# Second layer of a two-layer attention and expert backbone: units ordered by token group, vector work placed inside the attention stream

## The reference, cut to what matters

```
# modulation: m = silu(cond) @ w_mod + b_mod, six rows of 1024 per group
q, k, v = split(h @ w_in_c)                  # 1024 -> 1024 | 256 | 256
q, k = rms_norm per head of 64               # 16 query heads, 4 key heads
# g = 1 only: rotary on q and k; 128 cached keys and values are appended
o = softmax(q k^T / 8) v                     # g = 0: 128 keys, g = 1: 256 keys
x = layer_norm(ALPHA * x + gate * (o @ w_out_c))
h = modulate(x)                              # then router, 16 experts, top 2
y = sum over experts of gate_e * (silu(h w_gate) * (h w_up)) w_down
```

## Time and profile before

| | us |
|---|---|
| median of 3 runs | 865.54 (863.39 to 866.21) |
| the profiled execution | 865.44 |
| its span, first to last instruction | 863.6 |
| TensorE busy in it | 775.2 (90%) |
| VectorE busy | 233.3 (27%) |
| ScalarE busy | 151.4 (18%) |
| mean granted TensorE clock | 0.962 of full |
| transfers | 287.37 MB, 333 GB/s over the span |

### The profile page before, as it was taken

One profiled execution on the slowest core, in us unless ns is written; L12 is line 12 of the kernel. 1 busy time (PEld: TensorE's weight loads), 2 busy tenths in 40 slices (PEclk: granted clock), 3 DMA queues, 4 the chain that ended last, 5 costly groups with the idle time before them and its releaser, 6 DMA issues.

```text
span 863.6 us, 9955 instructions
## 1 busy us (share of the span) xinstructions
PE 775.2 (90%) x3765; PEld 371.1 (43%) x3765; DVE 233.3 (27%) x531; ACT 151.4 (18%) x389; POOL 63.3 (7%) x126
## 2 busy tenths in 40 slices
PE   4799788999999998797899996999999999997794
PEld 1345444546543443243234644554744434442331
DVE  0004444445210100000345055455610110000046
ACT  0211332213200111011112113233311101110120
POOL 0000000001100011001000030000200001101000
PEclk9898799999999999999999996999999999999998
DMA  8989940189999999999999899521099999999971
GB/s 312 382 311 401 389 152 31 68 307 404 419 419 417 420 419 417 419 422 414 417 386 384 321 353 420 227 98 64 35 370 417 420 416 419 421 415 418 419 321 50
DMA packets 78525, 287.37 MB, mean 333 GB/s; under 512 B 6508, under 2 KB 12140, under 8 KB 62100
## 3 DMA queue, kind: packets, MB, share of 16 engines
q1 hardware_dynamic: 74452, 275.60, 80.6%
q10 hardware_dynamic: 2880, 7.03, 2.1%
q0 software_dynamic: 1152, 4.19, 1.2%
HBM read 278.99 MB, written 7.82 MB: 332 GB/s over the span
## 4 chain that ended last, share of the span: by engine, by line
PE 50%; SPq 30%; DMA 7%; DVE 7%; issue 2%; ACT 2%; POOL 1%; ACTq 0%; DVEq 0%
SPq L580 15%; PE bank L1001 10%; SPq L575 9%; PE bank L748 9%; PE bank L837 6%; DMA ring<-in_exp_w_up 5%; SPq L576 4%; PE bank L1035 4%; PE bank L785 3%; PE bank L675 3%; DMA ring<-in_w_mod 2%; PE bank L654 2%; PE bank L972 2%; PE bank L816 2%; PE bank L794 2%
## 5 line engine op out<-in xcount | busy, mean ns | idle before, releaser
L1001 PE MATMUL bank<-ring,arena 128*64 128x512 f32 x1024 | 231.4, 605 | 30.1 <-DMA ring<-in_exp_w_up 29.2
L1001 PEld LDWEIGHTS bank<-ring,arena 128*64 128x64 f32 x1024 | 75.4, 139 | 182.8 <-issue 151.3
L1035 PE MATMUL bank<-ring,arena 128*64 128x512 f32 x512 | 113.8, 596 | 5.9 <-DMA ring<-in_exp_w_down 4.9
L1542 DVE TENSOR_TENSOR arena<-bank,arena 128x256 f32<-128x256 f32 x32 | 13.6, 424 | 253.6 <-ACT arena L1697 253.6
L748 PE MATMUL bank<-ring,arena 128*128 128x512 f32 (+2 forms) x224 | 75.4, 499 | 1.1 <-ACT arena L1631 1.1
L1621 ACT ACTIVATE arena<-bank 128x512 f32<-128x512 f32 (+6 forms) x79 | 41.0, 539 | 159.2 <-PE bank L748 66.9
L1035 PEld LDWEIGHTS bank<-ring,arena 128*64 128x64 f32 x512 | 36.1, 137 | 71.9 <-issue 64.6
L972 PE MATMUL bank<-arena 128*128 128x128 f32 x512 | 62.2, 275 | 0.0
L837 PE MATMUL bank<-ring,arena 128*128 128x512 f32 x128 | 60.3, 605 | 0.0
L972 PEld LDWEIGHTS bank<-arena 128*128 128x128 f32 x512 | 59.6, 192 | 1.3 <-issue 1.0
L675 PE MATMUL bank<-ring,cwin 128*32 128x512 f32 x384 | 48.2, 652 | 10.8 <-DMA ring<-in_w_mod 10.8
(11 more groups left out here) (168 smaller groups left out, 610.5 us busy)
## 6 DMA issues: line engine op xcount, KB each, us to landing
ring<-in_exp_w_gate SPq DMA_DIRECT2D x64, 1024.0 KB, 19.8
ring<-in_exp_w_up SPq DMA_DIRECT2D x64, 1024.0 KB, 20.6
ring<-in_exp_w_down SPq DMA_DIRECT2D x64, 1024.0 KB, 25.0
ring<-in_w_mod SPq DMA_DIRECT2D x24, 2048.0 KB, 18.2
expert_rows<-arena ACTq DMA_DIRECT2D x12, 512.0 KB, 7.8
ring<-in_w_out_ab SPq DMA_DIRECT2D x2, 2048.0 KB, 20.6
ring<-in_w_in_c SPq DMA_DIRECT2D x2, 2048.0 KB, 23.8
ring<-in_w_out_c SPq DMA_DIRECT2D x2, 2048.0 KB, 12.9
```

The source lines that it names most:

```text
L1001: mm = nc.tensor.matmul(pb(key)[SLOTS * hf:SLOTS * (hf + 1), :], xeT[b][:, k * P + SLOTS * a:k * P + SLOTS * (a + 1)], w[:, :, k % 4, hf * ...
L1035: mm = nc.tensor.matmul(pb(key)[SLOTS * a:SLOTS * (a + 1), :], hp[:, c:c + SLOTS], w[:, a, kf % 2, hf * HALF:(hf + 1) * HALF], start=(kf = ...
```

## The change

The second layer alone is changed; the first keeps its order.

- The units go by group: the four of g = 0 first, then the eight of g = 1.
- The projection goes by group: `project_odd` does all four blocks for g = 0, then for g = 1, so the first three blocks are given back later. The last block of g = 1 (the values) comes behind the transposes of g = 0's q and k (`odd_heads(0)`); that block is given back at the first scores.
- The two modulation pieces become four pairs (`mod_pair`), one before the first T and three behind T(1), T(2) and T(5); their closing matmul has 2 columns. Each pair gives its two ring slots back there.
- On DVE the scaling of g = 1 (`odd_scaled(1)`) stands behind T(0), the rotation, now in three pieces, behind T(1), the two residual sums of g = 0 behind T(5) and T(6), `mod_ab` and the normalisation of g = 0 behind T(7): each ahead of the next unit's maxima.
- q and k of g = 1 are turned behind T(2). The gates of g = 0 stand behind T(3) and T(4), the modulation's columns behind T(7), in bank 1, which the second residual sum has emptied. The columns of g = 0 for the router stand behind S(10) and S(11), its logits behind V(11).
- Of the four residual sums, the two of g = 1 are left behind the last Y, and the filler before the transposes there drops from five matmuls to three.

```diff
-    for pair in range((KVH_B if layer == 0 else KVH_C) // 2):
-        for g in range(G):
-            for kv in (2 * pair, 2 * pair + 1):
-                add("gqa", g, kv)
+    for g in range(G):
+        for kv in range(KVH_B if layer == 0 else KVH_C):
+            add("gqa", g, kv)
...
+    between = {0: [("n1", 0)], 1: [("mc", 1), ("n1", 1)], 2: [("mc", 2), ("g1", 0)], 3: [("gt", 0)], 4: [("gt", 1)],
+               5: [("mc", 3), ("au", 0)], 6: [("au", 1)], 7: [("mt", 0), ("nm", 0)]}
+    behind = {8: [("ht", 0)], 9: [("ht", 1)], 11: [("lg", 0)]}
     n = len(attention_units(layer))
     steps = [("S", 0), ("S", 1)]
+    if layer == 1:
+        steps.append(("mc", 0))
...
+        if layer == 1:
+            steps += between.get(u, [])
...
-        if layer == 0:
-            steps += make.get(u, [])
+        steps += (make if layer == 0 else behind).get(u, [])
...
-                for b in range(len(WIN[l])):
+                if l == 0:
+                    for b in range(len(WIN[l])):
+                        for g in range(G):
+                            t.use(("z", l, b, g), (2 * b + g) % 4)
+                    t.use(("mod", l, 1), 3)
+                else:
                     for g in range(G):
-                        t.use(("z", l, b, g), (2 * b + g) % 4)
-                t.use(("mod", l, 1), 3 - l)
-                if l == 1:
-                    t.use(("mod", 1, 2), 3)
+                        for b in range(len(WIN[l])):
+                            t.use(("z", l, b, g), b)
...
-                            t.use(("qT", 1, g, j), 4 + j)
-                    for j in range(2):
-                        t.use(("kT", 1, j), 6 + j)
+                            t.use(("qT", 1, g, j), (4 if g == 0 else 2) + j)
+                        t.use(("kT", 1, g), 6 if g == 0 else 2)
...
+                    elif name == "mc":
+                        t.use(step, 7)
+                    elif name == "gt":
+                        t.use(("gate", 1, 0, 0, u), 7)
+                    elif name == "mt":
+                        t.use(("modT", 1, 1), 1)
...
+            def project_odd():
+
+                for g in range(G):
+                    for b, (c0, c1) in enumerate(WIN[1]):
+                        if (g, b) == (1, 3):
+                            odd_heads(0)
+                        pe.wait_ge(*got(index[("win", 1, b)]))
+                        w = block_ap(index[("win", 1, b)])[:, 0:KD * (c1 - c0)].rearrange("p (k c) -> p k c", k=KD)
+                        key = ("z", 1, b, g)
+                        room(pe, key)
+                        if b == 0:
+                            pe.wait_ge(*saved(("hT", 1, 0, g, 1)))
+                            pe.wait_ge(*saved(("hT", 1, 0, g, 0)))
+                        for k in range(KD):
+                            mm = nc.tensor.matmul(pb(key)[:, 0:c1 - c0], hT[:, g, k, :], w[:, k, :],
+                                                  start=(k == 0), stop=(k == KD - 1))
+                            if (g, k) == (1, 0) and b > 0:
+                                mm.then_inc(*release(index[("win", 1, b - 1)]))
+                        mm.then_inc(*fill(key))
+
+            def odd_heads(g):
+
+                pe.wait_ge(s_zfin, 3 + g)
+                for a in range(2):
+                    transposes(("qT", 1, g, a), [z[1][:, g, (4 * a + j) * P:(4 * a + j + 1) * P] for j in range(4)])
+                keys = []
+                for a in range(2):
+                    keys.append(z[1][:, g, Z_KC + a * P:Z_KC + (a + 1) * P])
+                    if g == 1:
+                        keys.append(cache_kc[:, a * P:(a + 1) * P])
+                if g == 1:
+                    pe.wait_ge(s_cache, 96)
+                transposes(("kT", 1, g), keys)
+
+            def mod_pair(i):
+
+                key, first = ("mc", i), ODD_PAIRS[i]
+                room(pe, key)
+                out = pb(key)
+                for c in (first, first + 1):
+                    n = index[("mod", 1, c)]
+                    pe.wait_ge(*got(n))
+                    w = block_ap(n)
+                    for k in range(KD):
+                        j = k % 4
+                        mm = nc.tensor.matmul(out[32 * j:32 * j + 32, :], cwin[:, k, 24 - 2 * c:56 - 2 * c],
+                                              w[:, k * HALF:(k + 1) * HALF],
+                                              start=(c == first and k < 4), stop=False, skip_group_check=True)
+                    mm.then_inc(*release(n))
+                nothing = tri[0:DEPTH * N_MOD, 0:1].to_broadcast([DEPTH * N_MOD, 32])
+                nc.tensor.matmul(out[0:32, 0:2], nothing, rows[0:DEPTH * N_MOD, 0:2],
+                                 start=False, stop=True, skip_group_check=True).then_inc(*fill(key))
+
+            def odd_gate(hf):
+
+                pe.wait_ge(*saved(("mc", 0)))
+                mod_row(("gate", 1, 0, 0, hf), 1, 2, 0, hf)
+
+            def odd_columns():
+
+                for i in (1, 2):
+                    pe.wait_ge(*saved(("mc", i)))
+                mod_columns(1, 1)
+
...
+                    if (l, u, i) == (1, 0, 0):
+                        mm.then_inc(*release(index[("win", 1, 3)]))
...
-                        if (u, ci, hf) == (6, 0, 0):
+                        if (u, ci, hf) == (6 + 2 * l, 0, 0):
...
+                for g in range(l, G):
+                    logits(l, g)
...
-                project(l)
-                modulation(l, 1, (index[("win", l, len(WIN[l]) - 1)],))
-                if l == 1:
-                    modulation(1, 2)
+                if l == 0:
+                    project(0)
+                    modulation(0, 1, (index[("win", 0, len(WIN[0]) - 1)],))
+                else:
+                    project_odd()
...
+            def odd_rotated():
+                for h0, h1 in ((0, 8), (8, 16), (16, H_C + KVH_C)):
+                    last = rotate(halves(z[1][:, 1, h0 * HD:h1 * HD], h1 - h0), cst(C_COSB, 32), cst(C_SINB, 32),
+                                  odd_cos, odd_sin)
+                    if h1 < H_C + KVH_C:
+                        ch.then(last)
+                last.then_inc(s_zfin, 1)
+
...
+                odd_stats(0)
+                odd_scaled(0)
+                odd_stats(1)
+                odd_keys(0)
...
+                    elif name == "mc":
+                        dve.wait_ge(*full(step))
+                        if u > 0:
+                            dve.wait_ge(*saved(("mc", u - 1)))
+                        V.tensor_tensor(mods[1][:], mods[1][:], pb(step)[:], ALU.add).then_inc(*drain(step))
+                    elif name == "n1":
+                        (odd_rotated() if u else odd_scaled(1))
+                    elif name == "g1":
+                        odd_keys(1)
+                    elif name == "mt":
+                        mod_ab(1, 1)
+                    elif name == "au":
+                        add_up(1, 0, 0, u)
+                    elif name == "nm":
+                        normal(1, 0, 0)
...
                 if (l, s) == (1, 0):
-                    mod_ab(1, 1)
-                add_up(0, 0)
-                add_up(0, 1)
-                add_up(1, 0)
-                if (l, s) != (1, 1):
-                    normal(0)
-                add_up(1, 1)
+                    dve.wait_ge(s_out, 96)
+                else:
+                    add_up(l, s, 0, 0)
+                    add_up(l, s, 0, 1)
+                add_up(l, s, 1, 0)
+                if l == 0:
+                    normal(l, s, 0)
+                add_up(l, s, 1, 1)
...
+                        if g == 1:
+                            act.wait_ge(s_stat, root(("odd", 0)))
+                        for b in range(3):
                             act.wait_ge(*saved(("z", 1, b, g)))
-                        A.activation(sq[:, g].rearrange("p h c -> p (h c)"), z[1][:, g, 0:Z_VC],
+                        A.activation(sq.rearrange("p h c -> p (h c)"), z[1][:, g, 0:Z_VC],
                                      ACT.Square).then_inc(s_sq, 1)
-                    zp = z[1][:, 0, :]
-                    act.wait_ge(*saved(("z", 1, 3, 0)))
-                    act.dma_start(o_["new_gqa_v"][0, 0].rearrange("t h c -> t (h c)"),
-                                  zp[:, Z_VC:C_IN]).then_inc(s_out, 16)
+                        if g == 1:
+                            odd_queries(0)
+                        projected(1, 3, g)
```

243 lines of the change are left out of this document (131 added, 112 removed).

## The result

| | before | after |
|---|---|---|
| median of the runs | 865.88 us (4 runs) | 853.25 us (4 runs) |
| the profiled execution | 865.44 | 854.07 |
| its span | 863.6 | 852.3 |
| projection to first gate-and-up matmul | 161.50 | 147.21 |
| from there to the end of the span | 241.26 | 241.47 |

The ratio of after to before is 0.9838, with a 95% interval of 0.9805 to 0.9871. Forecast were 854.1 us and a first gate-and-up matmul near 611; it stands at 610.83.

A forecast was written before the change was run, and what follows sets the result against it. TensorE's list up to the second layer's first gate-and-up matmul was taken as the bound, with a fixed stretch behind it. 12.3 + 1.1 + 4.7 - 2.7 - 4.0 = 11.4 us gained, giving 854.1 us, range 850.5 to 860.

The forecast's parts named there:

- The frame: Second layer's first gate-and-up matmul sets the end: each microsecond earlier moves the whole remainder by one, 241 us to the end.
- The start of the attention: Second layer, before the first Y ends: waits for q, k and first softmax, and half clock, would go; gain 12.3 us.
- the closing matmuls: End of the modulation: two matmuls of 1.0 us each become four of two columns, 0.9 us together; gain 1.1 us.
- New waits: Second layer's attention: TensorE waits newly for DVE and ACT at several units; cost 4.0 us, bounds nothing to 18.7.
- The k transposes of g = 1: Behind the q transposes: TensorE waits 2.0 us for ACT's copy, held behind DVE's rotation and unit 3's exponentials.
- Y(0): First output tile, at 516.7: `w_out_c` lands at 516.3, so no wait was counted, with the cover nearly gone.
- The rival of a late weight: At the first output tile: `w_out_c` arrives late behind modulation blocks, 5 us, total 859 us; chance 0.07.
- the slow rival: Attention stream: DVE's queue becomes the bound and all 18.7 us of its work shows, total 871 us; chance 0.04.
- The end of the attention: Last Y to the transposes of g = 1: 10.87 us becomes 6.17 as two residual sums move earlier; gain 4.7 us.
- From those transposes to the experts: Transposes of g = 1 to first gate-and-up matmul, 19.2 us: led by DVE and GpSimd, so no gain counted.
- The logits: Router logits of g = 0 lengthen TensorE's stream by 1.75 us; with eight transposes, 0.93, the cost is 2.7 us.
- The rival of a falling clock: Inside the attention stream: TensorE's clock falls to half after a wait, price 3 us, total 857 us; chance 0.25.

The follow-up runs named there:

- e2: Changed kernel with all four modulation pairs put back ahead of the first scores; median 865.89 us, ratio to before 0.9995.
- e7: e1 with the second layer's units ordered by pair of key heads again instead of by group; median 861.19 us, ratio to before 0.9929.
- e8: e2 plus eight filler matmuls where TensorE waited, four ahead of T(0), four ahead of the q and k transposes of g = 1; median 865.33 us.
- e4: e3 with the transposes of g = 0 moved to the tail and one filler matmul instead of three before those of g = 1; median 853.24 us.
- e5: e3 with the output projection's first weight block two places earlier in the second layer's weight list; median 850.29 us.
- e1: Changed kernel with gates, modulation columns, residual sums, normalisation, transposes and logits of g = 0 put back at the end; median 855.85 us.
- e6: e5 with two filler matmuls instead of three ahead of the transposes of g = 1; median 850.88 us.
- e3: Changed kernel with only the logits of g = 0 moved back behind the transposes of g = 1; median 849.68 us, ratio to before 0.9809.

## Why the prediction was right, and where it was not

**The frame held.** The distance to the end is the same to 0.2 us in all fourteen profiles, so a microsecond of T is one of the total.

**The start of the attention, 12.3, and the closing matmuls, 1.1.** With the four waits as measured, 12.3 + 1.1 - 2.7 - 2.1 = 8.6, and the stream became 8.63 us shorter. Two small errors cancel in it: the four closing matmuls take 0.6 us (0.15 from 511.30 to 511.45), not 0.9, and the other matmuls of the pairs 14.3, not 14.0. e2 gives nearly all of it back, and e7 shows that the order by group is part of it. The prediction booked this gain as "waits for q, k and the first softmax, and half clock", all of which would go. It did not see what would set the time if the modulation were not there: DVE's list of 21 us from the first scores to the rotation's end, under which three pairs now lie. Nor was the half clock a loss by itself where that list was the longer one, as e8 showed.

**New waits, 4.0: this term was mis-sized; they are 2.1.**
- V(0): forecast 1.0, measured 0.88, behind the add at 511.55 and the copy at 512.16.
- The k transposes of g = 1: forecast 2.0, measured 0.34. The step that failed is mostly the rotation's place. It was put 58.4 us after the projection's start, with 6.6 us, and stood at 57.4 with 6.3, so its end came 1.3 us sooner; TensorE, held up at Y(0), came some 0.4 later. So ACT was through the exponentials when TensorE's transposes ended, and even waited for them, 0.27 us:

```profile
529.90 1.08 ACT L1740 ACTIVATE arena<-bank 128x512 f32<-128x512 f32 x2 [0.27 <-PE bank L842]
```

- V(7) and V(8): forecast 0.2 and 0.75, measured none and 0.32. So 2.1 of the 18.7 us of DVE's work that might have shown did, or less, since Y(0) is not DVE's. (The 18.7 has 4.5 for two residual sums that are 2.1 each; it should be 18.4, and only the upper bound and the slow rival's 871 rest on it.)
- Y(0): forecast nothing with its cover "nearly gone", measured 0.59 and 0.86, and up to 1.50 in e4. e5 showed that it is `w_out_c`. Its transfer was issued at 506.60, 43.0 us after the projection's start where the prediction had 42.6, and landed 12.9 us later, as forecast; TensorE was there at 519.04, 55.4 us after that start, not 55.9. The rival of a late weight had the place right and the price, 5 us, too high.

**The end of the attention, 4.7.** Measured 4.86 (10.87 to 6.01), confirmed by e1's 10.92. DVE was ready at 5.6, as e4 and e6 show, where 5.2 was forecast.

**From those transposes to the experts, "I count nothing".** Measured 0.8: 19.23 us became 18.43. This step failed in its reason, that this piece is led by DVE and GpSimd. Before, TensorE was the late one: sixteen transposes took 3.61 us (2.2 after), at a granted clock of 0.51, and the fillers behind them kept it until 613.55, while DVE had the chosen experts at 612.63. DVE and then TensorE, before:

```profile
612.44 0.19 DVE L1484 TENSOR_TENSOR chosen<-chosen,gsel 128x32 f32<-128x32 f32 x1
```

```profile
607.53 3.61 PE L732 MATMUL bank<-const,arena 128*128 128x128 f32 x16
...
613.55 0.30 PE L960 MATMUL bank<-chosen,const 128*128 128x32 f32 x2
```

After, the clock was 1.00 in this profile and the gain appeared; in the second profile of after it fell to 0.51 over the same transposes, and 19.18 us left next to nothing of the gain. So the 0.8 us are not to be counted on.

**The logits, 1.75 of the 2.7.** The term is right in size (1.81 measured), but e3 shows the price need not be paid: the tail has a wait of 1.55 us in which they fit.

**The rival of a falling clock** (chance 0.25) did not show where it was put: the stream was granted 1.00 in both profiles of after. The clock fell in the tail, for which the prediction had no term.

**The sum.** 14.3 us came from the stage, where 11.4 were forecast: 1.9 from the waits, 0.8 behind the transposes, 0.2 from the end of the attention. The profiled execution came out at 854.07 where 854.0 was forecast, and the first gate-and-up matmul at 610.83 instead of 611, because the untouched first layer ended 2.8 us later in it (463.62 against 460.84). Its end lay between 459.16 and 465.33 in the fourteen profiles. That these two numbers were hit is luck to this extent. The medians of all runs, 866.95 and 853.58, are 13.4 us apart, nearer to the 14.3 than to the 11.4.

**The exponential's table.** ACT after:

```profile
506.59 1.28 ACT L1784 ACT_TABLE_LOAD   x1
508.21 0.37 ACT L1784 ACTIVATE arena<-bank,negm 128x128 f32<-128x128 f32 x1 [0.33 <-DVE negm L1435]
```

ACT's copy ahead of the load ends at 506.57. The load is done at 507.87 and the first exponential starts 0.34 us later, when DVE's maxima are there, so the table cost nothing, as forecast. The Trainium skill, page "ScalarE: Activation LUTs", section "What ACT_TABLE_LOAD costs", gives 1.28 us for the load, as measured here, and 1.38 us of drain; neither ahead of the load nor behind it was there such a time in this trace.

## What to carry to other kernels

When one engine waits for another's list, measure how long that list is from the last thing it needs to the first thing it gives, and put as much independent work of the waiting engine inside it. Filling the gap with matmuls that compute nothing restores the clock in it and gains no time, since the list ends no earlier. Judge such a change by the stretch that it touches, in two profiles at least: here the untouched part moved by up to 6 us between executions, nearly half of the gain, and the tail by up to 2.4 us.

## What the runs showed of the hardware

The granted clock behind a run of narrow matmuls and transposes is not a property of the program alone: the same kernel (e5) was granted 1.00 and 0.87 over the same tail. In the tail each fall showed first in the 16-column logits or the transposes behind them. The Trainium skill, page "TensorE: Matmul & The Clock Gate", section "Part 4: PE-mode transpose", says that the full clock doesn't engage for transposes, as they don't count as busy in the same way as matmuls. These rows agree in that the falls lie there, and differ in that twelve of the same transposes also ran at a granted clock of 1.00 (1.51 us for 12, against 3.65 for 16 at 0.50). Nor are the slow rows transposes alone: in e4 and e5 the logits, matmuls behind eight transposes, were slow already (5.17 and 4.28 us instead of 3.64).
